# A conv and an attention block in one kernel: norms turned by a diagonal, attention in single steps, position biases in two loads, modulation ends three tiles later

## The reference, cut to what matters

```python
# block 1
mod = silu(c) @ mod_w + mod_b                    # sh1, sc1, g1, sh2, sc2, g2: six rows of 2048
h = rms_norm(x, norm1_g) * (1 + sc1) + sh1
u = h @ w_in; u = a * sigmoid(gate)              # 2048 -> 4096
u = depthwise_conv(u, 31 taps); u = silu(layer_norm(u))
x = x + (1 + g1) * (u @ w_out + b_out)
h = rms_norm(x, norm2_g) * (1 + sc2) + sh2       # the "first norm" of this document
x = x + (1 + g2) * (square(relu(h @ w1)) @ w2)   # 2048 -> 8192 -> 2048
# block 2
mod = silu(c_2) @ w_ada + b_ada
h = rms_norm(x, norm1_w) * (1 + sc1) + sh1       # the "second norm"
qa, ka, va, qb, kb, vb, ga, gb = split(h @ w_in) # 8 global heads (2 kv heads), 8 windowed heads
qa, ka = rope(rms_norm(qa)), rope(rms_norm(ka))
ya = softmax(qa ka^T / sqrt(128)) va
yb = softmax(qb kb^T / sqrt(128) + rpb[rows, cols]) vb   # window of 8 rows x 16 columns
x = x + g1 * ((sigmoid(ga) * (ya @ w_oa) + sigmoid(gb) * (yb @ w_ob)) @ w_out)
h = rms_norm(x, norm2_w) * (1 + sc2) + sh2       # the "third norm"
x = x + g2 * ((silu(h @ w_gate) * (h @ w_up)) @ w_down)  # 2048 -> 5632 -> 2048
return rms_norm(x, final_w)
```

## Time and profile before

| | |
|---|---|
| median of 3 runs | 2645.02 us (2641.45 to 2646.26) |
| profiled execution: its own time | 2643.18 us |
| span of its trace | 2641.1 us |
| mean granted TensorE clock | 0.983 of full |
| busy: TensorE | 2508.9 us (95%) |
| busy: VectorE, ScalarE, GpSimd | 1772.2, 1141.6, 371.5 us |
| HBM read, mean rate | 640.60 MB, 243 GB/s |
| SP queue, share of the 16 DMA engines | 74.4% |

### The profile page before, as it was taken

One profiled execution on the slowest core, in us unless ns is written; L12 is line 12 of the kernel. 1 busy time (PEld: TensorE's weight loads), 2 busy tenths in 40 slices (PEclk: granted clock), 3 DMA queues, 4 the chain that ended last, 5 costly groups with the idle time before them and its releaser, 6 DMA issues.

```text
span 2641.1 us, 29209 instructions
## 1 busy us (share of the span) xinstructions
PE 2508.9 (95%) x10688; PEld 1958.3 (74%) x10688; DVE 1772.2 (67%) x2150; ACT 1141.6 (43%) x1429; POOL 371.5 (14%) x177
## 2 busy tenths in 40 slices
PE   4899999899999999998999999999899999999998
PEld 2344557688887888886777788788688888888886
DVE  6679958667777778777664555695667654555455
ACT  2155445444443443444454454544444434443443
POOL 1069652022222222221000000000000000000000
PEclk9999999999999999999999999999899999999999
DMA  9999747488898988888745557886588766666664
GB/s 311 376 381 381 248 136 270 141 307 297 302 298 295 310 296 304 305 281 273 179 142 150 153 167 252 282 301 193 167 290 276 227 194 190 186 191 192 191 188 139
DMA packets 340157, 644.64 MB, mean 244 GB/s; under 512 B 30000, under 2 KB 63440, under 8 KB 338992
## 3 DMA queue, kind: packets, MB, share of 16 engines
q1 hardware_dynamic: 338752, 642.09, 74.4%
q0 software_dynamic: 448, 0.43, 0.1%
q10 hardware_dynamic: 816, 0.26, 0.1%
HBM read 640.60 MB, written 2.10 MB: 243 GB/s over the span
## 4 chain that ended last, share of the span: by engine, by line
PE 82%; DVE 10%; DMA 4%; ACT 2%; issue 1%; SPq 1%; POOL 0%; DVEq 0%; ACTq 0%; POOLq 0%
PE bank L86 82%; DVE bank L86 5%; DMA stage<-in_mod_w 3%; DVE wlo L86 1%; DVE R L86 1%; ACT whi L86 1%; DVE X L86 1%; DVE acc L86 1%; DVE scr L86 1%; SPq L86 1%; DMA stage<-in_conv_w_in 1%; DVE R2f L86 1%; ACT scr L86 0%; DMA stage<-in_w_in 0%; ACT hhi L86 0%
## 5 line engine op out<-in xcount | busy, mean ns | idle before, releaser
L86 DVE TENSOR_TENSOR wlo<-stage,whi 128x1024 fp32r<-128x1024 f32 x688 | 857.2, 1247 | 641.3 <-ACT whi L86 624.0
L86 ACT ACTIVATE whi<-stage 128x1024 fp32r<-128x1024 f32 x752 | 795.8, 1059 | 1023.6 <-PE bank L86 909.9
L86 PE MATMUL bank<-whi,hhi 128*128 128x512 f32 x2016 | 804.5, 399 | 24.3 <-DVE wlo L86 8.4
L86 PE MATMUL bank<-whi,hlo 128*128 128x512 f32 x2016 | 790.4, 392 | 0.0
L86 PE MATMUL bank<-wlo,hhi 128*128 128x512 f32 x2016 | 790.2, 392 | 0.0
L86 PEld LDWEIGHTS bank<-whi,hhi 128*128 128x128 f32 x2016 | 382.2, 190 | 111.0 <-ACT scr L86 15.3
L86 PEld LDWEIGHTS bank<-wlo,hhi 128*128 128x128 f32 x2016 | 382.2, 190 | 80.8 <-issue 3.1
L86 PEld LDWEIGHTS bank<-whi,hlo 128*128 128x128 f32 x2016 | 381.5, 189 | 81.3
L86 PE MATMUL bank<-whi,uhi 128*128 128x512 f32 x992 | 390.1, 393 | 2.1 <-POOL wlo L86 1.4
L86 PE MATMUL bank<-whi,ulo 128*128 128x512 f32 x992 | 389.8, 393 | 0.0
L86 PE MATMUL bank<-wlo,uhi 128*128 128x512 f32 x992 | 388.0, 391 | 0.0
(11 more groups left out here) (119 smaller groups left out, 1139.8 us busy)
## 6 DMA issues: line engine op xcount, KB each, us to landing
stage<-in_mlp_w SPq DMA_DIRECT2D x256, 512.0 KB, 5.5
stage<-in_mod_w SPq DMA_DIRECT2D x192, 512.0 KB, 9.1
stage<-in_w_ada SPq DMA_DIRECT2D x192, 512.0 KB, 5.5
stage<-in_w_in SPq DMA_DIRECT2D x136, 512.0 KB, 3.9
stage<-in_w_ffn_gate SPq DMA_DIRECT2D x88, 512.0 KB, 4.4
stage<-in_w_ffn_up SPq DMA_DIRECT2D x88, 512.0 KB, 4.4
stage<-in_w_ffn_down SPq DMA_DIRECT2D x88, 512.0 KB, 4.1
stage<-in_conv_w_in SPq DMA_DIRECT2D x128, 256.0 KB, 9.0
```

The source lines that it names most:

```text
L86: made = fn(*args, **kw)
```

## The change

1. *Norms.* The quarter is no longer scaled before it is transposed. `dg` holds, per token half, the identity times the reciprocal root, and `turn_quarter` multiplies X's 128x128 blocks (as the stationary side) by it: ordinary float32 matmuls. `modulate_first` handles quarter 0 column tile by column tile; the others follow with `later`: turn of quarter q at 2q - 2 tiles, modulation at 2q - 1. Turns 0 and 1 are issued before the first product tile. Three partial sums are added ahead (`partial_sums`), the fourth goes into the root's own instruction, and the last quarter is squared at once. Ten 128-column matmuls of constants (`N_WARM`) are issued ahead of the turn. At the last tile before a norm (`before_norm`) one weight pair less is prepared.
2. *Single steps.* `between_tiles` runs one of the `slow` list.
3. *Biases.* `load_biases` is put beside the 24th load after the first norm: two loads of 64 x 8 x 219 numbers into `R3`, from which `shifted_rows` reads with strides; the mask's load moves with them.
4. *Modulation.* Ends are due three tiles later, also where it was one (`L_SUMS`). No modulation tile stands in the first and last 6 of the MLP's tiles nor in the first 8 of the last stage; 32 stand on 44 tiles, 128 on 200.
5. *Head outputs.* Four heads are split at the last projection tile, before its epilogue; the others after it. The early root is left out in that stage.
6. *End.* Features 0 to 1535 are multiplied by `final_w` in the last stage (`times_final`); the reciprocal is applied by VectorE and ScalarE, and stores go out in the order of the quarters 0, 3, 1, 2.

```diff
@@ between_tiles
-            for _ in range(min(len(slow), 1 + len(slow) // 10)):
+            for _ in range(min(len(slow), 1)):
@@ consume
-                        later(L_SUMS if m["aside"] else 1, lambda m=m: mod_end(m))
+                        later(L_SUMS, lambda m=m: mod_end(m))
@@ norms
+        def partial_sums():
+            for tok in range(2):
+                t = V.put(nc.vector.tensor_reduce, ST[:, 8 + tok:9 + tok], ST[:, 4 * tok:4 * tok + 3], AX.X, ALU.add, ...)
+                partial[tok] = V.put(nc.vector.tensor_scalar, ST[:, 14 + tok:15 + tok], ST[:, 8 + tok:9 + tok],
+                                     1.0 / D, EPS, ALU.mult, ALU.add, ...)
+        def root_of(tok):
+            std[tok] = A.put(nc.scalar.activation, ST[:, 10 + tok:11 + tok], ST[:, 4 * tok + 3:4 * tok + 4], ACT.Sqrt,
+                             bias=ST[:, 14 + tok:15 + tok], scale=1.0 / D, after=[sumsq[(tok, 3)], partial[tok]])
+        def turn_quarter(q, made):
+            if misc.n_free() < 2:
+                later(1, lambda: turn_quarter(q, made))
+                return
+            two = [misc.take(), misc.take()]
+            t = {}
+            for tok in range(2):
+                for kk in (0, 2, 1, 3):
+                    _, bank, free = two[kk % 2]
+                    o = (kk // 2) * 256 + tok * 128
+                    xs = X[:, tok, (4 * q + kk) * 128:(4 * q + kk + 1) * 128]
+                    t[kk % 2] = T.put(nc.tensor.matmul, bank[:, o:o + 128], xs, dg[:, tok, :], start=True, stop=True,
+                                  after=[made[tok]] + free)
+        def modulate_first(n, ready, free_lhs):
...
+            shape(0)
+            shape(2)
+            for task, kk in ((high, 0), (shape, 1), (high, 1), (shape, 3), (high, 2), (high, 3)):
+                task(kk)
+            for kk in range(4):
+                lo = V.put(nc.vector.tensor_tensor, hlo[:, kk, :], part[kk], hhi[:, kk, :].bitcast(F32), ALU.subtract, ...)
+                ready[kk] = (hi[kk], lo)
@@ pe_tile
-                while len(pair_ready) < min(g - n_native + NPAIR, len(pe_list) - n_native):
+                ahead = NPAIR - (g in before_norm)
+                while len(pair_ready) < min(g - n_native + ahead, len(pe_list) - n_native):
@@ residual_epilogue
-                        if last:
+                        if last and q == 3:
+                            square_sum(tok, q, t)
+                            root_of(tok)
+                        elif last:
                             later(1, lambda tok=tok, t=t: square_sum(tok, q, t))
+                            if which == 5 and block == 1:
+                                later(2, lambda tok=tok: times_final(tok, q))
+                    if last and q == 2:
+                        later(3, partial_sums)
@@ streams
-        seq += mix(mlp, mods)
+        seq += mlp[:6] + mix(mlp[6:50], mods[:32]) + mix(mlp[50:-6], mods[32:]) + mlp[-6:]
-        seq += mix(ffn[:64], mods) + ffn[64:]
+        seq += ffn[:8] + mix(ffn[8:72], mods) + ffn[72:]
@@ load_biases
-            for h in range(8):
-                for rq in range(4):
-                    src = bass.AP(a["nat_rpb_2"].tensor, h * 465 + (7 - rq) * 31 + 15 - 63, [[1, 64], [31, 4], [1, 64]])
-                    t = Y.load(dst, src, ln_b, after=after)
+            for half in range(2):
+                src = bass.AP(a["nat_rpb_2"].tensor, (5 - half) * 31 + 15 - 63, [[1, 64], [465, 8], [1, N_RUN]])
+                rows_in = Y.load(R3[64 * half:64 * half + 64, 0, 0, 0:8 * N_RUN].rearrange("p (h n) -> p h n", h=8),
+                                 src, ln_b, after=[marks["bout_read"]])
@@ norm_phase
             flush()
-            r = rstd_of_sums()
+            made = []
+            for tok in range(2):
+                r = rstd_of(tok)
+                made.append(V.put(nc.vector.tensor_scalar, dg[:, tok, :], ident[:, :], ST[:, 12 + tok:13 + tok], None,
+                                  ALU.mult, after=[r, consts] + dg_read))
             while any((n, k, q) not in mod_cols for k in range(2) for q in range(4)):
                 run_one() if tasks or delayed or slow else consume()
-            for q in range(4):
-                tasks.append(lambda q=q: norm_quarter(n, q, r, ready, [lhs_read]))
+            b, bank, free = misc.take()
+            for _ in range(N_WARM):
+                t = T.put(nc.tensor.matmul, bank[:, 0:128], ones[:, :], ident[:, :], start=True, stop=True,
+                          after=[consts] + free)
+            misc.give(b, t)
+            turn_quarter(0, made)
+            modulate_first(n, ready, [lhs_read])
+            turn_quarter(1, made)
+            later(1, lambda: modulate_turned(n, 1, ready, [lhs_read]))
+            for q in (2, 3):
+                later(2 * q - 2, lambda q=q: turn_quarter(q, made))
+                later(2 * q - 1, lambda q=q: modulate_turned(n, q, ready, [lhs_read]))
@@ main
+        beside[loaded_upto[0] + 24] = load_biases
         products(n2, n3)
...
-        load_biases()
-        products(n3, n4)
+        def first_heads():
+            while slow:
+                slow.popleft()()
+            split_y(range(0, 4))
+        products(n3, n4, at_end=first_heads)
         flush()
-        split_y()
+        split_y(range(4, 16))
```

More of the change, by code:

```diff
@@ L34 @@
 L_SQUARE = 3
+N_RUN = 219
+N_WARM = 10
 L_JOB_END = 2
@@ L586, in scale_rows @@
             return scaled
-        def norm_quarter(n, q, rstd, ready, free_lhs):
-            scaled = scaled_rows.pop((n, q), None) or scale_rows(q, rstd)
-            cols = [mod_cols[(n, 0, q)], mod_cols[(n, 1, q)]]
[L593 to L601, removed]
+        turned = {}
@@ new lines, in modulate_first, with shape, high @@
+        def modulate_first(n, ready, free_lhs):
+            two, t = turned.pop(0)
+            cols = [mod_cols[(n, 0, 0)], mod_cols[(n, 1, 0)]]
+            bufs = [tiles.take(), tiles.take()]
+            part = [bufs[kk // 2][1][:, (kk % 2) * 256:(kk % 2) * 256 + 256] for kk in range(4)]
+            exact, hi = {}, {}
+            def shape(kk):
+                src = two[kk % 2][1][:, (kk // 2) * 256:(kk // 2) * 256 + 256]
+                sc, sh = MC[:, n, 0, kk:kk + 1], MC[:, n, 1, kk:kk + 1]
+                after = [t[kk % 2]] + cols + bufs[kk // 2][2]
+                if kk % 2:
+                    exact[kk] = A.put(nc.scalar.activation, part[kk], src, ACT.Identity, scale=sc, bias=sh, after=after)
+                else:
+                    exact[kk] = V.put(nc.vector.tensor_scalar, part[kk], src, sc, sh, ALU.mult, ALU.add, after=after)
+            def high(kk):
+                hi[kk] = A.put(nc.scalar.activation, hhi[:, kk, :], part[kk], ACT.Copy, after=[exact[kk]] + free_lhs)
+            shape(0)
[3 more added lines that the diff above has]
+            for kk in range(4):
+                lo = V.put(nc.vector.tensor_tensor, hlo[:, kk, :], part[kk], hhi[:, kk, :].bitcast(F32), ALU.subtract,
+                           after=[exact[kk], hi[kk]] + free_lhs)
+                ready[kk] = (hi[kk], lo)
+                if kk % 2:
+                    tiles.give(bufs[kk // 2][0], lo)
+            misc.give(two[0][0], exact[2])
+            misc.give(two[1][0], exact[3])
@@ L602, in norm_quarter, with modulate_turned @@
+        def modulate_turned(n, q, ready, free_lhs):
+            if q not in turned:
+                later(1, lambda: modulate_turned(n, q, ready, free_lhs))
+                return
+            two, t = turned.pop(q)
+            cols = [mod_cols[(n, 0, q)], mod_cols[(n, 1, q)]]
             e0, bufs = [], []
@@ L693, in build_program @@
         n_chunk = [0]
+        before_norm = []
         def pe_tile(g):
@@ L1401, in finish_bias @@
                 b, bank, free = misc.take()
-                t2 = T.put(nc.tensor.matmul, bank[:, :], flip[:, :], bias_of(h).rearrange("p t n -> p (t n)"),
-                           start=True, stop=True, after=[t, flips] + free)
+                for t in range(2):
+                    t2 = T.put(nc.tensor.matmul, bank[:, t * S:(t + 1) * S], flip[:, :], shifted_rows(h, t),
+                               start=True, stop=True, after=[rows_in, flips] + free)
+                marks["R3_free"] = marks["R3_free"] + [t2]
                 bias_ready[h] = V.put(nc.vector.tensor_tensor, bias_of(h),
@@ L1492, in build_program, with split_y @@
         yk_ready = {}
-        def split_y():
-            for h in range(16):
+        def split_y(heads):
+            for h in heads:
                 q = att[h]["q"]
@@ L1584, in build_program @@
         assert n6 == len(pe_list)
+        before_norm += [n2 - 1, n3 - 1, n5 - 1]
         def load_x():
@@ L1692, in build_program @@
         flush()
[L1693 removed]
         out_line = line("s_out")
         ov = out[0].rearrange("(t p) n -> t p n", p=128)
+        r = [rstd_of(tok) for tok in range(2)]
+        made = {}
         for tok in range(2):
[L1697 removed]
+            rstd = ST[:, 12 + tok:13 + tok]
```

(15 more changed lines are left out.)

35 lines of the change are left out of this document (26 added, 9 removed).

## The result

The changed kernel takes **2603.7 us** (median of 4, 2601.37 to 2609.94) against 2645.5; the ratio is 0.9849 (95% interval 0.9828 to 0.9869). The forecast was 2604.5. Its profiled execution has a span of 2600.4 us, 40.7 less than before, at a mean clock of 0.992 (before 0.983). (Line 88 is now the place where instructions are issued.)

A forecast was written before the change was run, and what follows sets the result against it. TensorE was taken to be at its floor in the long stages, so only its holes or half clock could pay: 2643.2 - 33.8 - 6.0 + 0.4 + 0 - 0.3 = 2603.5, stated as 2604.5 us, own range 2596 to 2611.

The forecast's parts named there:

- Norms, 33.8 us: Three norms: TensorE's lost time falls from 64.7 us together to 10.3 us per norm, saving 33.8 us.
- two covers that I called thin: Norms: held-back weight pair ready at L + 9.7, just when wanted; quarter 1 reached by about 11, due L + 12.5.
- Rival (b): Norms: the held-back weight pair or quarter 1 is late by 3 us in each norm, total 2613; chance 0.12.
- (d): Norm turns: a diagonal record's load and stream run one after the other, 6.6 us more per norm, 2624; chance 0.06.
- (e): Norm turns: (d) at a half clock that never recovers, 61 us more, 2665, slower than before; chance 0.04.
- rival (a): Norms: the clock falls all the same, 5.9 us more per norm, total 2622; chance 0.13.
- The hole of 1.1 us: Norms: TensorE idle some 1.1 us after the warm matmuls; taken as too short to lower the clock.
- Attention, 6.0 us: Attention in single steps: 7.6 us of waits and half clock go, 1.6 us of breaks come; 6.0 us saved.
- Head outputs, 0.4 us lost: Start of head outputs: third weight pair rounded about 1.1 us later, TensorE waits; 0.4 us lost, between 0.6 gained and 1.5 lost.
- Biases and modulation in the MLP, 0: MLP: loads hold SP at least 3.6 us, costing 0.8; later modulation ends take that back, net 0.
- Rival (c): MLP: weight supply limited to 301 GB/s, a tile takes 3.01 us rather than 2.76, 11 us over 44 tiles, 2616; chance 0.08.
- End, 0.3 us: End: only the first store's start counts, moving by about 0.3 us; the faster two-engine final scaling is worth nothing.

## Why the prediction was right, step by step

- *Norms, 33.8 us:* measured 33.8. The total is right; terms inside it are off and cancel, which is luck. I let the turn start when both diagonals are ready (L + 3.5) and the product at L + 7.0; the first token half's four blocks need only the first diagonal and start at L + 2.5, so the product starts at L + 6.2. Against that stand tile 1's wait of 0.44 us, one of the two covers that I called thin, and breaks of about 0.1 us around each turn. Rival (b), 3 us per norm, didn't come.
- *Price of a diagonal record:* 0.11 taken, 0.106 measured, the bound of the weight load. Rivals (d) and (e) fall with it. So does the factor of four between ordinary float32 matmuls and transposes that the Trainium skill states (TensorE: Matmul & The Clock Gate, Terms): here a turn of eight blocks costs 1.70 us against 0.79, little more than twice.
- *Clock:* full in all norms, in the nine traces with diagonals and warm matmuls in all 27, so rival (a) is out. Two reasons that I gave for it fell. The hole of 1.1 us that I allowed wasn't there, since the warm matmuls reach to the turn. That the clock survived 2.82 us in the attention proved nothing: with the steps undone it fell behind the same wait, and without the warm matmuls it fell once behind 1.9 us. I also said that the old trace agreed with what the Trainium skill states of transposes, that they don't count as busy (TensorE: Matmul & The Clock Gate, Part 4: PE-mode transpose). The old trace had lost its clock before the first transpose, and the run with transposes alone kept the full clock through all three norms, so in this kernel the traces do not agree.
- *Attention, 6.0 us:* 6.8 in the traces of before and after, 6.4 when it was undone alone. Two terms were off and cancel in part. The wait of 0.74 us, which I took back, stayed, against my "no wait over 0.5 us". And 20 more breaks (58 against 38 in this stage) cost next to nothing where I took 1.6: 5.3 us of waits and my estimate of 1.6 for the clock make 6.9 already.
- *Head outputs, 0.4 us lost:* 0.35, by the wait that was named (1.66 us at the third weight pair).
- *Biases and modulation in the MLP, 0:* +0.4 in the first trace. I scaled the hold on SP by rows to at least 3.6 us; the two loads held it 1.40 us, so the price doesn't go by rows alone. Their wait near 560 was one of my signs of being wrong; it came, at 0.49 us in the first trace and some 1.3 us in the mean, near my 0.8. Rival (c) would be seen as a pace of TensorE below its floor over 44 tiles; only single waits are there, and the transfers passed the 301 GB/s that it took for a limit (its 2.76 us per tile stands in no row either; the earlier trace rows give 2.72):

```profile
520.00:630.00 110.00, 108.89 (x490) 88.97 (x489) 84.06 (x76) 47.94 (x55) 26.83 (x10) 1.00 0.92 313
```

- *Second norm, 2.3 us for the 32 loads:* good enough for the difference between these two kernels, wrong as the price of the loads. With the shorter norm they would have cost 15.9.
- *End, 0.3 us:* 0.5, of which 0.3 are from the scaling that I had called worth nothing.

## What to carry to other kernels

When TensorE is at its floor, list the holes and sum what each loses against a fixed pace; such a sum forecast this change within 1 us, stage by stage, where medians scatter by 5, though some of its terms were off and cancelled. A wait that hides behind another has a price of its own: shortening the norms alone would have uncovered 14 us of a DMA queue held by small loads, so both had to go together. And the order in which a queue is filled decides whether an early result is used: under the old bodies an earlier root gained nothing, because weight remainders stood between it and the scaling; the gain came with turns issued ahead of the weight pairs.

## Unexpected of the hardware

- Float32 transposes kept the granted clock at 1.00 through 5.65 us without any product, three times of three in one trace; ordinary matmuls behind a hole of 1.9 us lost it once of three in another.
- Two scalings on VectorE take 0.88 us in the third norm, but 2.96 in the first, where GpSimd's remainder runs beside them (that this is the cause is not shown by a run of its own); both rows are of the run with the old norm bodies (VectorE, and GpSimd below):

```profile
499.50 2.96 DVE L88 TENSOR_SCALAR scr<-X,ST 128x512 f32<-128x512 f32 x2
```

```profile
499.33 2.45 POOL L88 TENSOR_TENSOR wlo<-stage,whi 128x1024 fp32r<-128x1024 f32 x1 [40.53 <-ACT whi L88]
```
